# One root for two norms in a row behind the second dense layer

## The reference

```
h = h + conv_ffn(rms_norm(h, norm_ffn[1]), ...)          # second dense layer
x = rms_norm(h, norm_final)                              # end of block one
# block two, layer 0
h = rmsnorm(x, ln1_g[0]) * (1.0 + sc1) + sh1
z = h @ w_in[0]
...
x = x + g1 * (concatenate([lru, att]) @ w_out[0])        # x, the first norm's result, is the residual
```

## Time and profile before

| what | value |
|---|---|
| three runs | 2078.46, 2081.14, 2083.44 us, median 2081.14 |
| the run with a profile | 2088.03 us |
| its span in the trace | 2086.2 us |
| mean granted TensorE clock | 0.985 of full |
| busy: TensorE, VectorE, ScalarE | 97%, 82%, 60% |
| DMA | 534.53 MB, 256 GB/s over the span |
| the stretch of the change | about 760 to 775 us |

### The profile page before, as it was taken

One profiled execution on the slowest core, in us unless ns is written; L12 is line 12 of the kernel. 1 busy time (PEld: TensorE's weight loads), 2 busy tenths in 40 slices (PEclk: granted clock), 3 DMA queues, 4 the chain that ended last, 5 costly groups with the idle time before them and its releaser, 6 DMA issues. The chain is left out here.

```text
span 2086.2 us, 31412 instructions
## 1 busy us (share of the span) xinstructions
PE 2030.1 (97%) x12388; PEld 1759.5 (84%) x12389; DVE 1717.7 (82%) x1983; ACT 1257.7 (60%) x1282; POOL 45.5 (2%) x84
## 2 busy tenths in 40 slices
PE   9999999999899999999999999999999999999998
PEld 8889997988799988799998878888888788888876
DVE  6868887886788877778788788988898889989997
ACT  5564447643444356643445777777777777777775
POOL 0000000000000000000000000000000000000000
PEclk9999999998899999999999999999999999999999
DMA  7358862201477644378874259998999899999995
GB/s 279 122 209 278 308 228 76 103 22 44 179 282 263 246 136 169 124 293 302 305 258 147 101 210 374 360 368 324 377 354 370 321 367 361 355 350 366 362 343 212
DMA packets 79466, 534.53 MB, mean 256 GB/s; under 512 B 11840, under 2 KB 13120, under 8 KB 15584
## 3 DMA queue, kind: packets, MB, share of 16 engines
q1 hardware_dynamic: 71744, 481.04, 62.3%
q0 software_dynamic: 7440, 51.49, 6.7%
q10 hardware_dynamic: 144, 0.02, 0.0%
HBM read 531.47 MB, written 1.05 MB: 255 GB/s over the span
## 5 line engine op out<-in xcount | busy, mean ns | idle before, releaser
L2454 DVE TENSOR_TENSOR weights_lo<-ring,weights_hi 128x2048 fp32r<-128x2048 f32 x193 | 436.7, 2280 | 64.0 <-ACT weights_hi L2448 63.7
L826 PE MATMUL bank<-acts_hi,weights_hi 128*128 128x256 f32 x1584 | 454.2, 287 | 6.3 <-DVE acts_lo L425 3.8
L403 DVE TENSOR_TENSOR weights_lo<-ring,weights_hi 128x2048 fp32r<-128x2048 f32 x161 | 368.0, 2290 | 110.0 <-ACT weights_hi L393 108.8
L393 ACT CAST weights_hi<-ring 128x2048 fp32r<-128x2048 f32 x161 | 307.0, 1908 | 249.5 <-PE bank L826 224.6
L826 PE MATMUL bank<-acts_lo,weights_hi 128*128 128x256 f32 x1584 | 448.1, 283 | 0.0
L826 PE MATMUL bank<-acts_hi,weights_lo 128*128 128x256 f32 x1584 | 448.0, 283 | 0.0
L2448 ACT CAST weights_hi<-ring 128x2048 fp32r<-128x2048 f32 x192 | 367.3, 1917 | 80.8 <-PE bank L2969 50.1
L826 PEld LDWEIGHTS bank<-acts_hi,weights_hi 128*128 128x128 f32 x1584 | 303.6, 192 | 14.6 <-issue 11.5
L2969 PE MATMUL bank<-weights_hi,xg_hi 128*128 128x512 f32 x768 | 305.3, 398 | 7.1 <-issue 3.3
L826 PEld LDWEIGHTS bank<-acts_lo,weights_hi 128*128 128x128 f32 x1584 | 303.8, 192 | 2.6 <-issue 1.4
L826 PEld LDWEIGHTS bank<-acts_hi,weights_lo 128*128 128x128 f32 x1584 | 303.8, 192 | 0.0
(11 more groups left out here) (500 smaller groups left out, 2869.8 us busy)
## 6 DMA issues: line engine op xcount, KB each, us to landing
ring<-in_experts SPq DMA_DIRECT2D x192, 1024.0 KB, 6.6
ring<-in_dense SPq DMA_DIRECT2D x162, 1024.0 KB, 4.9
ring_more<-in_experts SPq DMA_DIRECT2D x96, 1024.0 KB, 6.7
ada<-in_ada POOLq DMA_DIRECT2D x48, 1024.0 KB, 5.2
silu_c<-in_c SPq DMA_DIRECT2D x3, 512.0 KB, 6.4
resid<-in_x SPq DMA_DIRECT2D x2, 512.0 KB, 4.3
out<-resid SPq DMA_DIRECT2D x4, 256.0 KB, 2.1
small<-in_consts SPq DMA_DIRECT2D x1, 649.5 KB, 10.3
```

The costliest lines, as they stand in the source:

```text
L393: nc.scalar.copy(split[0][:, n % SPLITS, :], ring[:, n % RING, :]).then_inc(hi_ready, 1)
L403: nc.vector.tensor_tensor(split[1][:, n % SPLITS, :], ring[:, n % RING, :], split[0][:, n % SPLITS, :].bitcast(F32), ALU.subtract).then_in ...
L826: ins = nc.tensor.matmul(bank[:, f * T:(f + 1) * T], split[w][:, m % SPLITS, k * 256 + f * P:k * 256 + (f + 1) * P], acts[x][:, k, :], sta ...
L2454: ins = nc.vector.tensor_tensor(split[1][:, at, lo:hi], place(j)[0][:, lo:hi], split[0][:, at, lo:hi].bitcast(F32), ALU.subtract)
```

## The change

ScalarE keeps the first norm's mean (with eps) instead of its root: at h=1 an Identity takes the place of the Sqrt. VectorE makes from both means the one number under the second norm's root, in two operations on a column (`both_means`), and ScalarE takes one Sqrt of it (`roots`), which VectorE inverts and scales by. The first norm's root is a second Sqrt, issued right behind, and VectorE inverts it behind the scaling of both tiles. The squares of `xn` use the other tile's part of AT as scratch, at h=0 the Identity stands behind the second square, and TensorE runs 4 fillers ahead of the transposes where it ran 6.

```
 def half(t, h):
     act.wait_ge(summed, self.sums + 2 * t + h + 1)
     square(t, h, resid, 2 * t + h)
-    act.wait_ge(squares, done[0])
+    if h == 1:
+        act.wait_ge(squares, done[0])
+        mark(activation(stat[4 + t], stat[2 * t + 1], Identity, scale=1.0 / D, bias=stat[4 + t]))
+    act.wait_ge(normed, self.weighed + 2 * t + h + 1)
+    square(t, h, xn, 10 + 2 * t + h)
     if h == 0:
+        act.wait_ge(squares, done[0] - 1)
         mark(activation(stat[4 + t], stat[2 * t], Identity, scale=1.0 / D, bias=rms_eps))
-    else:
-        activation(stat[6 + t], stat[2 * t + 1], Sqrt, scale=1.0 / D, bias=stat[4 + t]).then_inc(rooted, 1)
-    act.wait_ge(normed, self.weighed + 2 * t + h + 1)
-    square(t, h, xn, 10 + 2 * t + h)

-def second_root(t):
+def roots(t):
     act.wait_ge(normed, self.weighed + 2 * TT + 3 * t + 1)
     act.wait_ge(squares, done[0])
-    mark(activation(stat[14 + t], stat[10 + 2 * t], Identity, scale=stat[16 + t], bias=rms_eps))
-    act.wait_ge(squares, done[0])
-    activation(stat[18 + t], stat[11 + 2 * t], Sqrt, scale=stat[16 + t], bias=stat[14 + t]).then_inc(rooted, 1)
+    activation(stat[18 + t], stat[11 + 2 * t], Sqrt, scale=1.0 / D, bias=stat[14 + t]).then_inc(rooted, 1)
+    activation(stat[6 + t], stat[4 + t], Sqrt).then_inc(rooted, 1)

 # VectorE
-def first_root(t):
-    dve.wait_ge(rooted, self.rooted + 2 * t + 1)
-    link(reciprocal(col(6, t), col(6, t)))
-    scalar_tensor_tensor(col(16, t), col(6, t), 1.0 / D, col(6, t), mult, mult).then_inc(normed, 1)
+def both_means(t):
+    dve.wait_ge(squares, self.squares + 6 * t + 5)
+    link(tensor_scalar(col(14, t), stat[10 + 2 * t], 1.0 / D, None, mult))
+    scalar_tensor_tensor(col(14, t), col(4, t), rms_eps, col(14, t), mult, add).then_inc(normed, 1)
-def second_root(t):
-    dve.wait_ge(rooted, self.rooted + 2 * t + 2)
+def scaled(t):
+    dve.wait_ge(rooted, self.rooted + 2 * t + 1)
     link(reciprocal(col(18, t), col(18, t)))
-    link(tensor_tensor(col(18, t), col(18, t), col(6, t), mult))
     for w in self.halves[t]:
         tensor_scalar(xn[:, t, w], xn[:, t, w], col(18, t), None, mult).then_inc(normed, 1)
 for t in range(TT):
-    first_root(t)
-    second_root(t)
+    both_means(t)
+    scaled(t)
+for t in range(TT):
+    dve.wait_ge(rooted, self.rooted + 2 * t + 2)
+    link(reciprocal(col(6, t), col(6, t)))

-norm.pe(pe, *((2, 3), (6, 2), (3, 2))[name])
+norm.pe(pe, *((2, 3), (4, 2), (3, 2))[name])
```

More of the change, by code:

```diff
@@ L652, in square @@
                     w = self.halves[t][h]
-                    mark(nc.scalar.activation(junk[:, t, w], src[:, t, w], ACT.Square, accum_out=stat[:, at:at + 1]))
+                    mark(nc.scalar.activation(junk[:, t if src is resid else 1 - t, w], src[:, t, w], ACT.Square, accum_out=stat[:, at:at + 1]))
                 def half(t, h):
@@ L657, in half @@
                     square(t, h, resid, 2 * t + h)
-                    act.wait_ge(squares, done[0])
+                    if h == 1:
+                        act.wait_ge(squares, done[0])
+                        mark(nc.scalar.activation(stat[:, 4 + t:5 + t], stat[:, 2 * t + 1:2 * t + 2], ACT.Identity, scale=1.0 / D,
+                                                  bias=stat[:, 4 + t:5 + t]))
+                    act.wait_ge(normed, self.weighed + 2 * t + h + 1)
+                    square(t, h, xn, 10 + 2 * t + h)
                     if h == 0:
+                        act.wait_ge(squares, done[0] - 1)
                         mark(nc.scalar.activation(stat[:, 4 + t:5 + t], stat[:, 2 * t:2 * t + 1], ACT.Identity, scale=1.0 / D,
                                                   bias=const("rms_eps")))
-                    else:
-                        nc.scalar.activation(stat[:, 6 + t:7 + t], stat[:, 2 * t + 1:2 * t + 2], ACT.Sqrt, scale=1.0 / D,
-                                             bias=stat[:, 4 + t:5 + t]).then_inc(rooted, 1)
-                    act.wait_ge(normed, self.weighed + 2 * t + h + 1)
-                    square(t, h, xn, 10 + 2 * t + h)
-                def second_root(t):
+                def roots(t):
                     act.wait_ge(normed, self.weighed + 2 * TT + 3 * t + 1)
                     act.wait_ge(squares, done[0])
-                    mark(nc.scalar.activation(stat[:, 14 + t:15 + t], stat[:, 10 + 2 * t:11 + 2 * t], ACT.Identity,
-                                              scale=stat[:, 16 + t:17 + t], bias=const("rms_eps")))
-                    act.wait_ge(squares, done[0])
-                    nc.scalar.activation(stat[:, 18 + t:19 + t], stat[:, 11 + 2 * t:12 + 2 * t], ACT.Sqrt,
-                                         scale=stat[:, 16 + t:17 + t], bias=stat[:, 14 + t:15 + t]).then_inc(rooted, 1)
+                    nc.scalar.activation(stat[:, 18 + t:19 + t], stat[:, 11 + 2 * t:12 + 2 * t], ACT.Sqrt, scale=1.0 / D,
+                                         bias=stat[:, 14 + t:15 + t]).then_inc(rooted, 1)
+                    nc.scalar.activation(stat[:, 6 + t:7 + t], stat[:, 4 + t:5 + t], ACT.Sqrt).then_inc(rooted, 1)
                 half(0, 0)
@@ L679, in act_rows @@
                 half(1, 0)
-                second_root(0)
+                roots(0)
                 half(1, 1)
-                second_root(1)
+                roots(1)
                 round_to(act, self.then + self.look)
@@ L686, in dve_rows @@
                 col = lambda i, t: stat[:, i + t:i + t + 1]
-                def first_root(t):
+                def both_means(t):
+                    dve.wait_ge(squares, self.squares + 6 * t + 5)
+                    dve_step.link(dve, nc.vector.tensor_scalar(col(14, t), stat[:, 10 + 2 * t:11 + 2 * t], 1.0 / D, None, ALU.mult))
+                    nc.vector.scalar_tensor_tensor(col(14, t), col(4, t), const("rms_eps"), col(14, t), ALU.mult, ALU.add).then_inc(normed, 1)
+                def scaled(t):
                     dve.wait_ge(rooted, self.rooted + 2 * t + 1)
-                    dve_step.link(dve, nc.vector.reciprocal(col(6, t), col(6, t)))
-                    nc.vector.scalar_tensor_tensor(col(16, t), col(6, t), 1.0 / D, col(6, t), ALU.mult, ALU.mult).then_inc(normed, 1)
-                def second_root(t):
-                    dve.wait_ge(rooted, self.rooted + 2 * t + 2)
                     dve_step.link(dve, nc.vector.reciprocal(col(18, t), col(18, t)))
-                    dve_step.link(dve, nc.vector.tensor_tensor(col(18, t), col(18, t), col(6, t), ALU.mult))
                     for w in self.halves[t]:
@@ L700, in dve_rows @@
                 for t in range(TT):
-                    first_root(t)
-                    second_root(t)
+                    both_means(t)
+                    scaled(t)
+                for t in range(TT):
+                    dve.wait_ge(rooted, self.rooted + 2 * t + 2)
+                    dve_step.link(dve, nc.vector.reciprocal(col(6, t), col(6, t)))
             def dve_columns(self, dve):
```

## The result

The changed kernel takes 2095.21 us (median of 5 runs) against 2081.14 us: a ratio of 1.0060, 95% interval 1.0047 to 1.0073. It is 14 us slower; forecast was 1.3 us faster, in a range that ended at 2083.4. One execution of e9 took 3351 us at a mean granted clock of 0.554 and is left out of its figures.

A forecast was written before the change was run, and what follows sets the result against it. TensorE, busy 97% of the span, was taken as the bound, with winnable waits in short stretches; the norms' t=1 chain, 1.32 us shorter, took the 2081.14 us median to 2079.8, range 2076.3 to 2083.4.

The forecast's parts named there:

- nothing behind the norm keeps an old time: After the norms, TensorE is busy throughout, so 1.32 us earlier at 774.81 is 1.32 us at the end.
- the most that this side can give: Two fillers fewer ahead of TensorE's transposes: 1.72 us as the upper limit of what that edit gives.
- The chain of t=1: Second tile's path through the two norms to its scaling and transposes sets the stretch's end; 1.32 us shorter.
- ScalarE's root of t=1: Second tile's Sqrt on ScalarE, expected at 768.88, a 0.03 us wait behind the square.
- VectorE's second mean: Second tile's column operation on VectorE, 0.16 us long; means ready 0.12 us ahead of ScalarE, so hidden by the square.
- the bounds of 0.7 to 1.4: Gain in us from the two norms, allowing for dearer or free roots and late means.
- the second Sqrt: First norm's own root on ScalarE at t=0, priced 0.11 us, with 0 and 0.29 as bounds.
- the reciprocals: Two of 0.19 us for the residual, moved behind VectorE's last scaling; hidden, with 0.19 to spare.
- a gain that is taken up: Rival: stretch ends earlier but a later independent wait sets the next layer; no change, 2081.1 us, chance 0.12.
- The clock: Rival: fewer fillers let TensorE's clock fall between 768.4 and the next layer's first blocks; 1.78 us lost, 2081.6, chance 0.13.
- the norm at 880 us: Norm with two fillers, 0.66 us of waiting and 16 transposes ran at clock 1.00; evidence against a clock fall.
- The range: Whole-kernel time of 2076.3 to 2083.4 us, from the clock's 2083.4 and some 2.5 us of scatter about 2079.8.

The follow-up runs named there:

- e9: The kernel before with 8 narrow fillers instead of 10 at the start of the program, norms untouched: 2094.01 us, ratio 1.0074.
- e1: The kernel before with 4 fillers instead of 6 ahead of the transposes, old norms kept: 2095.12 us, ratio 1.0063.
- e3: The changed kernel, still 4 fillers ahead, plus two fillers of 8 columns (eight instructions) behind the transposes: 2082.98 us, ratio 1.0005.
- e6: The changed kernel with one filler of 8 columns (four instructions) added behind the transposes: 2094.38 us, ratio 1.0064.

## Why the prediction was wrong

**The step that failed** is the last one of the sum, "nothing behind the norm keeps an old time", so that "1.32 us earlier at 774.81 is 1.32 us at the end". I priced the two fillers by their time (1.72 us, "the most that this side can give") and looked for what starts earlier on engines and queues. I left out that they are eight instructions of TensorE's program, and that code which lies 650 us behind them in time moves by eight places. What stood in the place of that step is a second stall of 4.27 and 4.42 us at the two jumps back, with a low clock behind each: 6.9 and 6.5 us. e1 shows that this edit carries the whole loss, e3 that eight instructions put in behind the transposes take it back, and e9 that the norm has no part in it. The trace of before had a sign: TensorE's waits for issue at L2969, 1.48 and 1.79 us, two of them, the only ones over 0.5 us, and a DMA queue for instructions. I read the chain for the end of the stretch and not for what the stretch's instructions push.

The Trainium skill, "Runtime: NRT & Kernel Launch", section Instruction fetch mechanics, has the rule: code is fetched in blocks of 16 KiB (256 instructions), and a taken jump to a target outside the window stalls for a fetch. The trace agrees with both, in 16384-byte packets and in 1.0 to 1.8 us at each jump. The same section of the Trainium skill calls the cost of crossing a block's end mostly hidden. Right behind a jump it is not, as the 4.27 us show.

**The chain of t=1** was right in kind. Its scaling starts 4.53 us behind the last projection matmul where I had 4.42, and 5.74 before: 1.21 us shorter, not 1.32. ScalarE's root of t=1 came 0.10 behind its square and not 0.03, which is most of the difference. VectorE's second mean took 0.22 and not 0.16 and ended 0.04 ahead of that square, where I had 0.12; which of the two held the root is not told. Behind it 0.21 more went: the two scalings of t=1 took 1.02 us together and not 0.88, and the first bank and the conversion came that much later. 1.00 us in all, within the bounds of 0.7 to 1.4.

**The rest of the norm** went as forecast: the second Sqrt cost 0.09 to the next instruction (0.11), the reciprocals are hidden, TensorE waits half a us for t=1, and six fillers let through 0.24 (0.2 to 0.3 by my working). The 1.0 us was carried on by the blocks that follow: beside the second profile of before, the changed trace gains 1.1 us at the norms and keeps it up to 1200 us. There, about the router's norm, it falls back by 1.0, with a clock of 0.79 from 1200 to 1216 us where the other has 0.89 from 1198 to 1214. e1, with the old norm, falls back there as well, and the written-out changed kernel does not (0.89), so this is no sign of a gain that is taken up. That the gain reaches the end is not shown by any median.

**The clock** did not fall in the norms in any run: with eight transposes, a wait of 0.52 us, and eight more between fillers it stayed at 1.00. The Trainium skill, "TensorE: Matmul & The Clock Gate", Part 4 (PE-mode transpose), says that transposes don't count as activity of TensorE in the same way. No effect of that shows in this stretch. The clock did fall with the second stalls, for a price of 1.9 us at the first and 1.7 at the second (14 matmuls in 4.88 us). The prediction leaned on the norm at 880 us, where the clock stayed; the same trace has a fall just ahead of it, near 868 us, behind eight transposes and a wait of 2.22 us. The second profile of before has no fall at that place. Falls of this kind, in one execution and not in the next, are worth as much as the whole forecast gain.

**The range** missed because every case in it was one of the next 20 us. A cause of 14 us was not among the rivals. Three slips in its working changed little: 2.5 us of scatter below 2079.8 end at 2077.3 and not at 2076.3, the cases lie within 2.3 us of 2081.14 and not 4.2, and the six entries of 4.52 us in the earlier trace rows are three fillers of two passes each, not six.

## What to carry to other kernels

An instruction added to or taken from an engine's program moves all code behind it; where a loop's head follows, work out how many instructions lie between the head and the end of its packet, and look at the waits for issue at the head and at the packets of the instruction queue before and after. When two versions of something small are compared, keep the number of instructions ahead of the loop equal, or write the loop out, or the comparison measures the place of the code. A pad of a few short instructions in a wait that exists anyway is a cheap way to move a loop's head.

## What the runs showed of the hardware

At nearly every jump back the packet after the head's starts 5.8 to 6.3 us after the head's own (1432.70 and 1438.79 in the changed kernel, 1436.83 and 1443.05 before, 1430.96 and 1437.09 in e6), whether TensorE stalls or not; the one exception is the second jump in the first profile of before, with 5.06 (1650.20 and 1655.26). In straight code packets mostly follow each other by 9 to 33 us. Near 478 us, where TensorE runs matmuls of 32 columns one behind the other, they follow by 3.3 to 5.9 us, and no wait of its matmuls for issue in straight code is over 0.5 us. Why the second packet behind a jump starts no earlier, though TensorE stands still for want of it, these runs don't tell; the DMA share was 0.98 meanwhile in the changed kernel, and no run has the same jump with idle DMA engines. Behind the second stall of the first jump the changed kernel ran at a granted clock of 0.52, near the lower level of 1.2 GHz; before, without that stall, the clock there was 1.00 and matmuls kept their 0.23 us spacing.
